# Sample key pages released by the count of projection chunks, six memory samples in two buffers, and two square roots moved on ScalarE

## The chip, the cores and the metric

The kernel runs on one core of a Trainium2 chip. Its time is the time on the device in microseconds (us), and the time of a version is the median of several runs.

## The reference

The kernel computes one layer of a decoder for a prompt of 256 tokens and for 8 samples of one token each. Both share the weights. Cut to what matters here:

```
h = rms_norm(x, norm1_w)
z = h @ w_in                                    # 2048 x 13312
zb, zc, zx, zq, zk, zv, zmq, zg = split(z)
y_conv = (zb * short_conv(zc * zx)) @ w_conv_out
q, k   = rope(rms_norm(zq)), rope(rms_norm(zk))
# prompt: attention over itself; sample: over 2048 cached positions (16 pages of 128) and itself
y_diff = subln(diff_attn(q, k_all, v_all)) @ w_diff_out
mk, mv = memory_kv(mem)                         # prompt: (rms_norm(mem) @ w_mem_kv), 256 memory rows
y_mem  = mem_attn(rms_norm(zmq), mk, mv) @ w_cross_out   # sample: its own cached 256 memory rows
x = x + (sigmoid(zg) * [y_conv, y_diff, y_mem]).sum() @ w_o
x = x + peer_ffn(rms_norm(x))                   # top 16 of 16384 experts for each of 8 heads, rows gathered
```

## The kernel before

All is fp32. The program is written engine by engine with semaphores; nothing is scheduled by a planner, so each engine and each DMA queue runs its list in the order in which it is written.

**Projections on TensorE.** `linear` computes z transposed in chunks of 128 columns for all 264 tokens. Four chunks make a cycle: `half_chunk(0, ...)` runs the first 8 of 16 contraction steps for the four chunks, and `half_chunk(1, ...)` the last 8. Each half reads one 2048 KB piece of weights in `wring`. SyncE fetches these pieces (`stream_halves`, `fetch_half`): the first half's buffer is refilled as soon as the four first halves are done, so its fetch runs during the second half of the cycle; the second half's buffer is refilled at the end of the cycle. `chunk_full` counts finished chunks, and it only moves in the second half of a cycle, once for each chunk. Chunks 1 to 8 are the queries, 9 to 16 the keys, 17 to 32 values and memory queries, 33 to 56 the three parts of the short convolution (`C_CONV` = 32). Then come 8 chunks of the prompt's memory (`C_MEM` = 56, 512 columns wide, L789), then the gates (L802, L814).

**Sample keys.** GpSimd's queue loads the 128 cached key pages, 512 KB each, in 32 groups of four (`load_pages`), into eight buffers: `kpages` 0 to 3 lie in `ring4`, 4 to 7 in `mkv`. A page is loaded when `kpage_used` says that the page eight before it was read. The index of the page is read from the table with `value_load`. VectorE multiplies a page by the broadcast query (L1510) and sums by head (L1515). Before each fourth group the query row of the next sample is loaded too.

**Memory scan.** After the pages, the 8 samples are scored against their cached memory in the same way (`score_memory`, L1540, L1543), two pages for a sample. `MEM_PAIR` says which pair of `kpages` a sample's two pages use. Each scored sample, of pages and of memory, moves `token_done`, which begins at 2; so 2+TS is the end of the page scan and 2+2*TS that of the memory scan (TS = 8).

**What waits for these.** The prompt's memory chunks are copied from PSUM into `mkv` by ScalarE (`memory_chunk`, L1190), and so can't be before the scan has left the pages in `mkv`. TensorE has four banks for the eight memory chunks, and chunk 5 needs chunk 1 taken. After chunk 8 TensorE runs `conv_state`, which needs VectorE's `conv_ready`, and `own_scores`, which needs all memory chunks taken.

**Roots.** VectorE's normalisations ask ScalarE for a square root: VectorE signals `sqrt_in` and waits for `sqrt_out` (L1473 is the instruction behind that wait); `root(n, ...)` on ScalarE is the other side. Root 3 belongs to the queries, root 4 to the keys and memory queries, root 5 to the prompt's memory keys.

The lines of the changed place:

```
for n in range(8):
    act.wait_ge(s["chunk_full"], C_QKV + 8 + n + 1)
    ...
    if n == 0:
        root(3, small[:, 3, 0:48])
...
conv_chunks(0, 5)
root(4, small[:, 3, 0:60])
conv_chunks(5, 1)
act.wait_ge(s["token_done"], 2 + 2 * TS)
```

Of the kernel before, what the change touches and what calls it, by code (L numbers as in the profile page):

```python
# [24 lines left out]
TP, TS = 256, 8  # L25
# [50 lines left out]
def build(nc, A, O):  # L76
# [17 lines left out]
    with ctx:  # L94
        def sb(name, shape, dt=F32):
            return ctx.enter_context(nc.sbuf_tensor("sb_" + name, shape, dt))

        def sem(name):
            return ctx.enter_context(nc.semaphore(name))
# [29 lines left out]

        kpages = [ring4[:, n, :] for n in range(4)] + [sq_mkv[:, n * DC:(n + 1) * DC] for n in range(4)]  # L130
        ring_flat = ring4[:, :, :].rearrange("p a b -> p (a b)")
        MEM_PAIR = [2, 3, 0, 1] * 2

        scores = cflat[:, 0:3 * 2 * PH * NKEY].rearrange("p (t n) -> p t n", t=3)
        work = S[:, :, :, :].rearrange("p a b c -> p (a b c)")
# [65 lines left out]
        small = sb("small", [P, 5, P])  # L201
# [18 lines left out]
        s = {n: sem(n) for n in names}  # L220
# [11 lines left out]
        C_QKV, C_CONV, C_MEM, C_O, C_PQ = 0, 32, 56, 64, 80  # L232
# [26 lines left out]
        def u_slot(g, j):  # L259
            return g * TOPK + j + dots_after(g, j - 1)  # L260
# [137 lines left out]
        def _(pool):  # L398
# [35 lines left out]
            pool.wait_ge(s["small_in"], 80)  # L434
            pool.wait_ge(s["xT_kept"], 16)

            def load_pages(i, g):

                par, half = g // 4 % 2, g % 2
                if g % 4 == 0:  # L440

                    b = i * 2 + g // 4
                    pool.wait_ge(s["token_done"], i * 2 + (g // 4 + 1))
                    pool.dma_start(qb[:, par, :], q_dram[ds(b, 1), :].to_broadcast([P, DC])).then_inc(qb_landed[par], 16)
                for r in range(4):
                    n = i * 32 + (g * 4 + r)
                    pool.wait_ge(s["kpage_used"], n + 1)
                    page = pool.value_load(pt[0:1, ds(n, 1)], min_val=0, max_val=POOL_PAGES - 1)
                    pool.dma_start(kpages[4 * half + r], cache_k[ds(page * PAGE, PAGE), :]).then_inc(k_landed[4 * half + r], 16)
# [5 lines left out]
            def load_query(b):  # L455
                pool.dma_start(qb[:, b % 2, :], mq_dram[b:b + 1, :].to_broadcast([P, DC])).then_inc(qb_landed[b % 2], 16)

            def load_memory(b):
                for t in range(2):
                    n = 2 * MEM_PAIR[b] + t  # L460
                    pool.dma_start(kpages[n], cmem_k[b * NM + t * P:b * NM + (t + 1) * P, :]).then_inc(k_landed[n], 16)
# [18 lines left out]
            for b in range(2, TS):  # L480
                pool.wait_ge(s["token_done"], 2 + TS + (b - 2) + 1)
                load_query(b)
                if b + 2 < TS:
                    load_memory(b + 2)

            def load_page(p):

# [100 lines left out]
            for g in range(2 * PH):  # L588
                pool.wait_ge(s["idx_ready"], g + 1)
                st(nc.gpsimd.tensor_copy(uidx[:, g % 4, :], idx_flat[:, g * TOPK:(g + 1) * TOPK]))  # L590
                for j in range(TOPK):
                    n = u_slot(g, j)
# [3 lines left out]
                    if dots_after(g, j) > dots_after(g, j - 1):  # L596
                        b = dots_after(g, j - 1)
# [498 lines left out]
        def _(act):  # L1096
# [10 lines left out]
            def root(n, ap):  # L1107
                act.wait_ge(s["sqrt_in"], n)
                st(A_(ap, ap, ACT.Sqrt))
                act.sem_inc(s["sqrt_out"], 1)  # L1110
# [44 lines left out]

            to_stage(8, C_QKV, R_QKV)
            act.wait_ge(s["rows_taken"], R_QKV + 8 + 2)
            for n in range(8):
                act.wait_ge(s["chunk_full"], C_QKV + 8 + n + 1)
                st(A_(zst[:, n % 2, :], ps[:, n % 4, 0:NT], ACT.Copy))  # L1160
                act.sem_inc(s["chunk_taken"], 1)
                if n == 0:
                    root(3, small[:, 3, 0:48])
                for k in (2 * n, 2 * n + 1):
                    act.wait_ge(s["xT_full"], KC + k + 1)
                    st(A_(memT[:, k, :], ps[:, 6 + k % 2, 0:NM], ACT.Copy, scale=cols[:, KC + k:KC + k + 1]))
                    act.sem_inc(s["xT_taken"], 1)
                act.wait_ge(s["tr_full"], R_QKV + 8 + n + 1)
                at = slice(DC + n * P, DC + (n + 1) * P)
                st.run(A_(rows[:, 0:2, at], ps[:, 4 + n % 2, 0:2 * P].rearrange("p (t n) -> p t n", t=2), ACT.Copy))  # L1170
                st(A_(rows[0:TS, 2, at], ps[0:TS, 4 + n % 2, 2 * P:3 * P], ACT.Copy))
                act.sem_inc(s["rows_taken"], 1)
            to_rows(16, C_QKV + 16, R_QKV + 16, rows, 2 * DC)

            def conv_chunks(i0, n):
                with st.loop(n, 4) as i:
                    for q in range(4):
                        act.wait_ge(s["chunk_full"], i * 4 + (C_CONV + 4 * i0 + q + 1))
                        st(A_(cflat[:, ds(i * (4 * NT) + (4 * i0 + q) * NT, NT)], ps[:, q, 0:NT], ACT.Copy))
                        act.sem_inc(s["chunk_taken"], 1)  # L1180

            conv_chunks(0, 5)
            root(4, small[:, 3, 0:60])
            conv_chunks(5, 1)

            act.wait_ge(s["token_done"], 2 + 2 * TS)
            def memory_chunk(n):
                g, t = n // 2, n % 2
                act.wait_ge(s["chunk_full"], C_MEM + n + 1)
# [191 lines left out]
        def _(dve):  # L1381
# [151 lines left out]
            def score_memory(b):  # L1533
# [3 lines left out]
                for t in range(2):  # L1537
                    n = 2 * MEM_PAIR[b] + t
                    dve.wait_ge(k_landed[n], 256 + 16 * (MEM_PAIR[:b].count(MEM_PAIR[b]) + 1))
                    st.run(TT(prods[t], kpages[n], qb[:, par, :], ALU.mult))  # L1540
# [556 lines left out]
```

## Time and profile before

| | before |
|---|---|
| median of 3 runs | 2750.24 us (2749.55 to 2758.01) |
| the profiled execution, its own time | 2760.93 us |
| its span | 2759.3 us |
| TensorE busy | 2447.8 us (89%) |
| VectorE busy | 1493.1 us (54%) |
| GpSimd busy | 907.5 us (33%) |
| ScalarE busy | 351.2 us (13%) |
| DMA | 919.23 MB, mean 333 GB/s |

The shares are averages over stages that differ much: until some 1400 us TensorE is busy nearly all the time, and after that the gathers of the experts fill the DMA engines. The time of a stage is read from that stage's own stretches and waits.

### The profile page before, as it was taken

Reading aid. Unit: us, or ns where it says so; the run is one execution under the profiler, and the core shown is the slowest. Engines: PE = TensorE matmul, PEld = TensorE weight load, DVE = VectorE, ACT = ScalarE, POOL = GpSimd, SP = SyncE. Lnnn points to the kernel's source line nnn. Section 1 sums busy time; section 2 is a strip of 40 time slices with the busy share of each in tenths; the row PEclk is TensorE's granted clock in tenths of the full one; section 3 lists DMA queues with packets and bytes.
Section 4 is the critical chain, followed back from the end, with each engine's and each line's share of the span. In section 5 each row is a group of like instructions: output and inputs, shape, how many; then the busy total and the mean of one; then the engine's idle time right before and its main releaser. Section 6 shows DMA issues by size and latency. Waiting matters only on the chain.

```text
span 2759.3 us, 27121 instructions
## 1 busy us (share of the span) xinstructions
PE 2447.8 (89%) x8853; PEld 1522.5 (55%) x8853; DVE 1493.1 (54%) x2370; ACT 351.2 (13%) x773; POOL 907.5 (33%) x889
## 2 busy tenths in 40 slices
PE   9999989999999999999997778776999597777777
PEld 7877778358766678888885233332434143323333
DVE  3499997713322223012377877884554665555543
ACT  2111000012222210001112101111011011111110
POOL 1122221100122210000056565655544564455542
PEclk9999999999999999999998999998989899999999
DMA  6599995754799975447398999999999999999998
GB/s 224 192 385 375 364 357 211 299 198 156 246 355 346 349 251 186 137 140 257 122 362 339 422 416 417 419 412 421 421 408 422 414 414 414 418 417 421 421 422 372
DMA packets 269027, 919.23 MB, mean 333 GB/s; under 512 B 15738, under 2 KB 122322, under 8 KB 199892
## 3 DMA queue, kind: packets, MB, share of 16 engines
q0 software_dynamic: 122448, 725.64, 65.5%
q1 hardware_dynamic: 146468, 192.20, 20.5%
q8 instruction: 59, 0.97, 0.1%
q14 instruction: 52, 0.43, 0.0%
HBM read 909.08 MB, written 8.72 MB: 333 GB/s over the span
## 4 chain that ended last, share of the span: by engine, by line
PE 47%; DMA 28%; DVE 12%; POOL 7%; issue 5%; ACT 0%; SPq 0%; DVEq 0%; POOLq 0%; ACTq 0%
DMA sb_bregion<-in_peer_u_dram,sb_ring 13%; PE ps L802 13%; PE ps L695 11%; PE ps L814 6%; DMA sb_wring<-in_w_in_dram 6%; PE ps L687 4%; PE ps L789 4%; DMA sb_mkv<-in_peer_u_dram,sb_ring 3%; DMA sb_S<-in_peer_u_dram,sb_ring 3%; DVE sb_bregion L1995 3%; PE ps L1051 3%; PE ps L902 2%; DVE sb_mkv L1995 2%; DMA sb_bregion<-in_peer_v_dram,sb_ring 1%; POOL sb_bregion L556 1%
## 5 line engine op out<-in xcount | busy, mean ns | idle before, releaser
L1051 PE MATMUL ps<-sb_wring,sb_ring 128*128 128x512 f32 x992 | 454.3, 607 | 85.3 <-DMA sb_wring<-in_peer_v_dram,sb_ring 84.7
L695 PE MATMUL ps<-sb_hT,sb_wring 128*128 128x264 f32 x1792 | 420.0, 395 | 24.7 <-DMA sb_wring<-in_w_in_dram 24.7
L1995 DVE CUSTOM_DVE_ANT_0 sb_bregion<-sb_bregion,sb_rows 128x2048 f32<-128x2048 f32 x128 | 293.5, 2293 | 214.8 <-DMA sb_bregion<-in_peer_u_dram,sb_ring 207.6
L695 PEld LDWEIGHTS ps<-sb_hT,sb_wring 128*128 128x128 f32 x1792 | 346.0, 195 | 88.7 <-issue 18.1
L1051 PEld LDWEIGHTS ps<-sb_wring,sb_ring 128*128 128x128 f32 x992 | 185.2, 193 | 352.3 <-issue 255.1
L802 PE MATMUL ps<-sb_hT,sb_wring 128*128 128x264 f32 x1536 | 365.5, 389 | 1.6 <-DVEq L1387 1.6
L802 PEld LDWEIGHTS ps<-sb_hT,sb_wring 128*128 128x128 f32 x1536 | 287.1, 190 | 64.9 <-issue 16.4
L1051 PE MATMUL ps<-sb_oreg,sb_ring 128*128 128x512 f32 x496 | 237.7, 630 | 75.3 <-DMA sb_oreg<-in_peer_v_dram,sb_ring 55.4
L1051 PE MATMUL ps<-sb_hT,sb_ring 128*128 128x512 f32 x496 | 231.7, 614 | 54.1 <-DMA sb_hT<-in_peer_v_dram,sb_ring 45.5
L556 POOL DMA_INDIRECT sb_bregion<-in_peer_u_dram,sb_ring x132 | 174.4, 1321 | 219.8 <-DVEq L1387 183.5
L1354 ACT ACTIVATE sb_ring<-sb_ident,sb_ring 128x128 f32<-128x128 f32 x248 | 99.6, 402 | 915.0 <-PE ps L1051 781.0
L1051 PEld LDWEIGHTS ps<-sb_oreg,sb_ring 128*128 128x128 f32 x496 | 97.1, 202 | 215.0 <-issue 154.9
L1995 DVE CUSTOM_DVE_ANT_0 sb_S<-sb_S,sb_rows 128x2048 f32<-128x2048 f32 x64 | 146.7, 2293 | 111.0 <-DMA sb_S<-in_peer_u_dram,sb_ring 107.9
L1995 DVE CUSTOM_DVE_ANT_0 sb_mkv<-sb_mkv,sb_rows 128x2048 f32<-128x2048 f32 x64 | 147.1, 2298 | 104.3 <-DMA sb_mkv<-in_peer_u_dram,sb_ring 99.6
L1051 PEld LDWEIGHTS ps<-sb_hT,sb_ring 128*128 128x128 f32 x496 | 93.2, 195 | 191.3 <-issue 150.1
L556 POOL DMA_INDIRECT sb_wring<-in_peer_v_dram,sb_ring x128 | 165.1, 1290 | 50.9 <-issue 40.4
L556 POOL DMA_INDIRECT sb_mkv<-in_peer_u_dram,sb_ring x66 | 101.0, 1530 | 190.5 <-DVEq L1387 176.7
L1515 DVE TENSOR_REDUCE sb_S<-sb_oreg 128x1024 f32 x128 | 149.5, 1208 | 0.0
L556 POOL DMA_INDIRECT sb_S<-in_peer_u_dram,sb_ring x66 | 94.8, 1436 | 86.0 <-DVEq L1387 59.0
L814 PE MATMUL ps<-sb_oreg,sb_bregion 128*128 128x264 f32 x512 | 122.1, 388 | 0.0
L590 POOL COPY sb_ring<-sb_ring 128x16 int32<-128x16 int32 x16 | 16.7, 1047 | 309.4 <-DVEq L1387 309.3
L789 PE MATMUL ps<-sb_wring,sb_bregion 128*128 128x512 f32 x256 | 111.8, 599 | 6.5 <-DMA sb_wring<-in_w_mem_kv_dram 6.5
(367 smaller groups left out, 2595.6 us busy)
## 6 DMA issues: line engine op xcount, KB each, us to landing
sb_wring<-in_w_in_dram SPq DMA_DIRECT2D x52, 2048.0 KB, 13.6
sb_ring<-in_cache_k_dram POOLq DMA_DIRECT2D x64, 512.0 KB, 7.6
sb_mkv<-in_cache_k_dram POOLq DMA_DIRECT2D x64, 512.0 KB, 7.2
sb_mkv<-in_cache_v_dram POOLq DMA_DIRECT2D x48, 512.0 KB, 7.1
sb_rows<-in_cache_v_dram POOLq DMA_DIRECT2D x47, 512.0 KB, 7.7
sb_wring<-in_w_mem_kv_dram SPq DMA_DIRECT2D x8, 2048.0 KB, 8.4
sb_wring<-in_w_o_dram SPq DMA_DIRECT2D x8, 2048.0 KB, 8.2
sb_S<-in_cache_v_dram POOLq DMA_DIRECT2D x22, 512.0 KB, 7.2
```

The costliest lines, as they stand in the source:

```text
L556: nc.gpsimd.indirect_dma_start(dst, None, table, bass.IndirectOffsetOnAxis(ap=idx, axis=0)).then_inc(landed, 16)
L590: st(nc.gpsimd.tensor_copy(uidx[:, g % 4, :], idx_flat[:, g * TOPK:(g + 1) * TOPK]))
L687: last = mm(ps[:, (2 * r + c) % 4, 0:NT], wring[:, r, k, c * P:(c + 1) * P], rhs[:, k, :], start=(k == 0), stop=(k == KC - 1))
L695: last = mm(ps[:, c, 0:NT], whalf[:, h, k % BC, c * P:(c + 1) * P], rhs[:, k, :], start=(k == 0), stop=(k == KC - 1))
L789: last = mm(ps[:, 2 * g + t, :], memT[:, k, t * P:(t + 1) * P], whalf[:, h, k % BC, :], start=(k == 0), stop=(k == KC - 1))
L802: last = mm(ps[:, c, 0:NT], wring[:, r, k, c * P:(c + 1) * P], hT[:, k, :], start=(k == 0), stop=(k == KC - 1))
L814: last = mm(ps[:, bank, 0:NT], bwring[:, r, k, c * P:(c + 1) * P], operand[:, k, :], start=(k == 0), stop=(k == BC - 1))
L902: last = mm(ps[g * QUAD:g * QUAD + w.shape[1], 6 + q, :], w, v_slots[page_slot(p)][:, q * 512:(q + 1) * 512], start=first, stop=final)
L1051: last = mm(ps[:, 4 * t + q, :], diag[:, k % 4, :], e_slots[v % ER][:, q * 512:(q + 1) * 512], start=False, stop=q_stop, skip_group_check= ...
L1354: st(A_(diag[:, k % 4, :], ident[:, :], ACT.Copy, scale=wexp[:, g % 4, j:j + 1]))
L1515: st.run(RED(out(p), by_head(prods[p % 2]), X, ALU.add))
L1995: st(V.tensor_tensor_reduce(out=u_slots[n % UR], in0=u_slots[n % UR], in1=h2, scale=1.0, scalar=0.0, op0=ALU.mult, op1=ALU.add, accum_out= ...
```

## The change

It has four parts.

1. **Pace.** Before each group g of `load_pages(i, g)`, GpSimd's queue also waits for `chunk_full` to reach i*11 + 11 + floor(11*(g-2)/8). In numbers, the 32 groups wait for chunks 8, 9, 11, 12, 13, 15, 16, 17, then the same plus 11 (19, 20, 22, 23, 24, 26, 27, 28), plus 22 (30 to 39) and plus 33 (41, 42, 44, 45, 46, 48, 49, 50).
2. **Pairs of the memory scan.** Samples 0 and 1 still use pairs 2 and 3 (in `mkv`); samples 2 to 7 take turns in pairs 0 and 1 (in `ring4`). The pages of samples 4 to 7 are therefore loaded when the sample two before them has been scored, where before they were loaded when the sample four before had been.
3. **Memory chunks.** ScalarE waits for `token_done` of 2+TS+2 (two memory samples scored) before it copies memory chunk 1, where it waited for 2+2*TS.
4. **Roots.** Root 3 stands ahead of key chunk 9 and no longer behind it. Root 4 stands behind all 24 convolution chunks and no longer ahead of the last four.

```diff
-        MEM_PAIR = [2, 3, 0, 1] * 2
+        MEM_PAIR = [2, 3] + [0, 1] * 3
...
+            PACE = 11
+
             def load_pages(i, g):
...
                     pool.dma_start(qb[:, par, :], q_dram[ds(b, 1), :].to_broadcast([P, DC])).then_inc(qb_landed[par], 16)
+                pool.wait_ge(s["chunk_full"], i * PACE + (C_QKV + 11 + PACE * (g - 2) // 8))
                 for r in range(4):
...
                 load_query(b)
-                if b + 2 < TS:
-                    load_memory(b + 2)
+                if b >= 4:
+                    load_memory(b)
...
             act.wait_ge(s["rows_taken"], R_QKV + 8 + 2)
+            root(3, small[:, 3, 0:48])
             for n in range(8):
                 act.wait_ge(s["chunk_full"], C_QKV + 8 + n + 1)
                 st(A_(zst[:, n % 2, :], ps[:, n % 4, 0:NT], ACT.Copy))
                 act.sem_inc(s["chunk_taken"], 1)
-                if n == 0:
-                    root(3, small[:, 3, 0:48])
...
-            conv_chunks(0, 5)
+            conv_chunks(0, 6)
             root(4, small[:, 3, 0:60])
-            conv_chunks(5, 1)
-
-            act.wait_ge(s["token_done"], 2 + 2 * TS)
+
+            act.wait_ge(s["token_done"], 2 + TS + 2)
```

ScalarE, between the last query chunk and the first key chunks; L1160 (L1164 in the changed kernel) copies a key chunk out of PSUM, L1109 (L1112) is the root. Before:

```order
L69 COMPARE_AND_BRANCH
L1160 ACTIVATE sb_zst<-ps 128x264 [waits chunk_full,rows_taken]
L1109 ACT_TABLE_LOAD [waits act_done]
L1109 ACTIVATE sb_small<-sb_small 128x48 [waits sqrt_in]
L1166 ACTIVATE sb_bregion<-ps,sb_cols 128x256 [waits act_done,xT_full] x2
L1170 ACTIVATE sb_rows<-ps 128x2x128 [waits act_done,tr_full]
```

And now:

```order
L69 COMPARE_AND_BRANCH
L1112 ACT_TABLE_LOAD [waits sqrt_in]
L1112 ACTIVATE sb_small<-sb_small 128x48 [waits rows_taken]
L1164 ACTIVATE sb_zst<-ps 128x264 [waits act_done,chunk_full]
L1168 ACTIVATE sb_bregion<-ps,sb_cols 128x256 [waits act_done,xT_full] x2
L1172 ACTIVATE sb_rows<-ps 128x2x128 [waits act_done,tr_full]
```

The root and its table load moved ahead of the first key chunk; nothing else moved here.

GpSimd's queue, the memory scan's loads behind the stores of the prompt's keys and values; `mq_rows_scratch` is the memory query row of one sample, `in_cache_mem_k_dram` two pages of its memory. Before:

```order
L475 DMA out_v_prompt_dram<-sb_rows 128x2x1024
L477 DMA out_v_sample_dram<-sb_rows 8x1024
L456 DMA sb_oreg<-mq_rows_scratch 128x1024 [waits token_done]
L461 DMA sb_mkv<-in_cache_mem_k_dram 128x1024 x2
L456 DMA sb_oreg<-mq_rows_scratch 128x1024 [waits token_done]
L461 DMA sb_mkv<-in_cache_mem_k_dram 128x1024 x2
L456 DMA sb_oreg<-mq_rows_scratch 128x1024 [waits token_done]
L461 DMA sb_ring<-in_cache_mem_k_dram 128x1024 x2
L456 DMA sb_oreg<-mq_rows_scratch 128x1024 [waits token_done]
L461 DMA sb_ring<-in_cache_mem_k_dram 128x1024 x2
L456 DMA sb_oreg<-mq_rows_scratch 128x1024 [waits token_done] x2
```

And now:

```order
L478 DMA out_v_prompt_dram<-sb_rows 128x2x1024
L480 DMA out_v_sample_dram<-sb_rows 8x1024
L459 DMA sb_oreg<-mq_rows_scratch 128x1024 [waits token_done] x3
L464 DMA sb_ring<-in_cache_mem_k_dram 128x1024 x2
L459 DMA sb_oreg<-mq_rows_scratch 128x1024 [waits token_done]
L464 DMA sb_ring<-in_cache_mem_k_dram 128x1024 x2
L459 DMA sb_oreg<-mq_rows_scratch 128x1024 [waits token_done]
L464 DMA sb_ring<-in_cache_mem_k_dram 128x1024 x2
L459 DMA sb_oreg<-mq_rows_scratch 128x1024 [waits token_done]
L464 DMA sb_ring<-in_cache_mem_k_dram 128x1024 x2
```

The four pairs of pages moved two samples later in the queue, and all go to `ring4`.

## Rows read from the trace of the kernel before

**Rows 1.** Stretch of the gates to the scores: length, busy of each engine, PEclk, DMA, GB/s

```profile
595.00:1400.00 805.00, 801.77 (x4046) 629.81 (x4047) 211.52 (x468) 123.31 (x250) 94.76 (x163) 1.00 0.68 237
```

**Rows 2.** Stretches by cycle of four chunks; last columns PEclk, DMA share, GB/s

```profile
147.40:184.70 37.30, 33.48 (x146) 27.71 (x144) 36.88 (x33) 4.64 (x14) 9.07 (x18) 0.91 1.02 396
...
219.60:250.80 31.20, 29.99 (x142) 25.20 (x141) 30.78 (x28) 3.69 (x12) 7.51 (x15) 1.00 1.01 379
250.80:283.00 32.20, 29.93 (x141) 25.16 (x140) 31.26 (x29) 3.69 (x12) 7.96 (x15) 1.00 0.98 372
283.00:312.80 29.80, 29.42 (x135) 24.46 (x132) 29.80 (x27) 2.63 (x8) 7.78 (x15) 1.00 1.00 373
312.80:348.70 35.90, 30.57 (x128) 25.50 (x128) 35.48 (x33) 1.62 (x5) 8.69 (x17) 0.90 0.97 357
...
447.60:476.00 28.40, 28.40 (x129) 24.27 (x128) 18.63 (x17) 1.82 (x5) 6.17 (x11) 1.00 0.59 202
```

**Rows 3.** TensorE's waits, 120 to 480 us, and two of them in the timeline

```profile
PE ps L695 <- DMA sb_wring<-in_w_in_dram: 24.3, 9, 5.3
```

```profile
267.84 7.39 PE L695 MATMUL ps<-sb_hT,sb_wring 128*128 128x264 f32 x32 [2.27 <-DMA sb_wring<-in_w_in_dram]
...
317.95 30.57 PE L695 MATMUL ps<-sb_hT,sb_wring 128*128 128x264 f32 x128 [5.27 <-DMA sb_wring<-in_w_in_dram]
```

**Rows 4.** DMA issues of weights, median us to landing, 53 to 116 us

```profile
sb_wring<-in_w_in_dram SPq DMA_DIRECT2D x5, 2048.0 KB, 7.9
```

**Rows 5.** The same, weights and pages, 131 to 419 us

```profile
sb_wring<-in_w_in_dram SPq DMA_DIRECT2D x17, 2048.0 KB, 17.1
...
sb_ring<-in_cache_k_dram POOLq DMA_DIRECT2D x60, 512.0 KB, 7.8
```

**Rows 6.** Timeline of VectorE around root 3 and the first page

```profile
105.25 0.45 DVE L1473 RECIPROCAL sb_small<-sb_small 128x48 f32<-128x48 f32 x1 [11.72 <-ACTq L1110]
...
128.09 1.23 DVE L1510 TENSOR_TENSOR sb_oreg<-sb_ring,sb_oreg 128x1024 f32<-128x1024 f32 x1 [12.40 <-DMA sb_ring<-in_cache_k_dram]
```

**Rows 7.** VectorE's page multiplies from `ring4`: ns min/median/max, first and last start

```profile
L1510 DVE TENSOR_TENSOR sb_oreg<-sb_ring,sb_oreg x64: 1210/1216/1226, 128.1 to 411.3; 128x1024 f32<-128x1024 f32 x64
```

**Rows 8.** Timeline of GpSimd: first page of groups 10 and 24

```profile
205.59 0.53 POOL L449 DMA_DIRECT2D sb_ring<-in_cache_k_dram  x1 [4.02 <-DVEq L1387]
...
334.28 0.53 POOL L449 DMA_DIRECT2D sb_ring<-in_cache_k_dram  x1 [1.36 <-DVEq L1387]
```

**Rows 9.** Timeline of ScalarE: copies of chunks 22 and 41

```profile
212.80 0.39 ACT L1148 ACTIVATE sb_zst<-ps 128x264 f32<-128x264 f32 x1 [0.18 <-ACT sb_rows L1153]
...
372.48 0.39 ACT L1179 ACTIVATE sb_conv<-ps 128x264 f32 x1 [23.44 <-PE ps L695]
```

**Rows 10.** Timelines of ScalarE and VectorE around root 4

```profile
448.29 0.25 ACT L1109 ACTIVATE sb_small<-sb_small 128x60 f32<-128x60 f32 x1 [0.25 <-ACT sb_conv L1179]
```

```profile
448.62 0.53 DVE L1473 RECIPROCAL sb_small<-sb_small 128x60 f32<-128x60 f32 x1 [10.47 <-ACTq L1110]
```

**Rows 11.** VectorE's memory scan: first multiplies of sample 4; last sums

```profile
505.07 2.36 DVE L1540 TENSOR_TENSOR sb_oreg<-sb_mkv,sb_oreg 128x1024 f32<-128x1024 f32 x2 [1.51 <-DMA sb_oreg<-mq_rows_scratch]
...
524.61 2.34 DVE L1543 TENSOR_REDUCE sb_Sm<-sb_oreg 128x4 f32<-128x1024 f32 x2
```

**Rows 12.** ScalarE: first copy of memory chunks, root 5, first copy behind it

```profile
527.04 1.49 ACT L1190 ACTIVATE sb_mkv<-ps,sb_stat 128x512 f32<-128x512 f32 x2 [50.61 <-DVEq L1387]
...
554.74 0.21 ACT L1109 ACTIVATE sb_small<-sb_small 128x8 f32<-128x8 f32 x1 [14.89 <-DVEq L1387]
```

**Rows 13.** The page's DMA issues: memory pages, median us to landing

```profile
sb_mkv<-in_cache_mem_k_dram POOLq DMA_DIRECT2D x8, 512.0 KB, 11.7
```

**Rows 14.** TensorE in the memory chunks and at the first gate chunk

```profile
475.84 13.90 PE L789 MATMUL ps<-sb_wring,sb_bregion 128*128 128x512 f32 x32
496.20 97.86 PE L789 MATMUL ps<-sb_wring,sb_bregion 128*128 128x512 f32 x224 [6.46 <-DMA sb_wring<-in_w_mem_kv_dram]
...
595.29 7.39 PE L802 MATMUL ps<-sb_hT,sb_wring 128*128 128x264 f32 x32
```

## The prediction, on record before the changed kernel ran

> **What bounds the kernel now.** I read the stretches by engine first, then TensorE's waits, then the landings of the DMAs that end them. From the gates to the scores TensorE is busy 801.77 of 805.00 us at a granted clock of 1.00 [rows 1]. What shortens the time up to the first gate chunk at 595.29 us [rows 14] is therefore worth its full size there, and the gathers behind it start by so much earlier, unless some later transfer needed the time. So the question is when the first gate chunk starts.
>
> Up to there TensorE loses time while key pages are loaded. The stretches by cycle show it: a cycle of four chunks takes 28.40 us at the end, when no page is in flight, and 37.30, 31.20, 32.20, 29.80, 35.90 us in the scan [rows 2]. A clean cycle of the first 32 chunks is 31.20 less its one wait of 1.2, or 29.9; 32.20 less 2.27 says the same [rows 2, 3]. The first convolution cycle is 29.5. The ten cycles from 147.40 to 476.00 would take 4 x 29.9 + 29.5 + 5 x 28.4 = 291.1 us clean and take 328.6. **The loss is 37.5 us**, of which 24.3 us are nine waits for weights [rows 3], and the rest is slow running behind the long ones: the stretch with the wait of 5.27 has a granted clock of 0.90, the one with 2.27 has 1.00 [rows 2, 3]. A wait of 2 us costs itself, one of 5 us about 7.
>
> Why the weights are late: a piece of 2048 KB lands 7.9 us after its issue when nothing else moves [rows 4] and 17.1 us in the scan [rows 5], and its due time is half a cycle, 14.2 to 15 us. Pages are read by VectorE at (411.3 - 128.1) / 123 = 2.30 us each [rows 7], 9.2 us a group, so 3.1 groups in a clean cycle.
>
> **Root 3.** VectorE waits 11.72 us for root 3, from 93.53 to 105.25 [rows 6], because ScalarE first waits for key chunk 9. In the new order only the table load and the root lie between, about 1.8 us from the same row's neighbours, so the query rows, their way through DRAM and the first page come some 9.9 us earlier: first multiply at 118.2 in place of 128.09 [rows 6]. ScalarE was idle there; the cost is nothing. But it isn't a gain by itself: VectorE is not what TensorE waits for. It brings the first collision one cycle forward, into the piece fetched at some 116 us. I charge the 7.4 us that the first cycle with pages loses now (37.30 - 29.9) [rows 2] to the new first one, and 2 us (bounds 0 and 5) to the next, since the pace doesn't hold in either.
>
> **Pace.** Groups ask for 11 chunks in 8 groups, 1.375 chunks of 7.1 us or 9.8 us a group in a clean run, against 9.2 by VectorE. It doesn't hold for the first ten groups. Group 10 was issued at 205.59 and would now wait for chunk 22, copied at 212.80; group 24 was issued at 334.28 and would wait for chunk 41, copied at 372.48 [rows 8, 9]. So the pages fall back behind the chunks, to three groups in a cycle and two in the cycles of chunks 29 to 32 and 49 to 52. All are released in the second half of a cycle, at chunk 1 of it at the earliest. The piece fetched at the start of that half has 3.6 us and the page's own latency to itself, half of its 7.9 us [rows 4]; the rest shared as now at half speed gives some 12 us of the 14.2. The piece fetched at the end of the cycle meets what is left of the second group and the whole third. In bytes a conv cycle now wants 4.2 MB of weights, 6.3 of pages and 0.4 of query rows, 10.9 MB in 28.4 us or 384 GB/s, against 372 to 396 GB/s moved in the busiest cycles [rows 2]. That is tight. Bounds: no wait at all, or two in three of the later cycles with 2.3 us each and a slow one (15 us in all). I take 6 us, nearest to the row with 2.27, since a wait that short left the clock alone.
>
> Sum for the end of the convolution chunks: 37.5 - 7.4 - 2 - 6 = **22.1 us earlier**, at 453.9.
>
> **Root 4.** It now stands behind chunk 56: 453.9 + 1.0 (as 448.62 stands to the end of chunk 52 at 447.60 [rows 2, 10]). VectorE asks for it 26.9 us after the last multiply from `ring4` (438.15, from 448.62 - 10.47, less 411.3) [rows 7, 10]. Group 30 is released by chunk 49 at 414.8, its page lands by 7.8 us [rows 5], four pages take 6.9: VectorE asks at about 456. Root and request meet; the reciprocal comes at 456, 7.4 us later than now.
>
> **Memory scan.** Samples 2 to 7 live on two pairs. Now four samples take 526.95 - 505.07 = 21.9 us, 5.5 each [rows 11]. With the load issued when the sample two before is done, a sample takes half of landing plus scoring: (7.8 + 4.7) / 2 = 6.25 [rows 5, 11]; over four samples +3. The memory pages' median is 11.7 [rows 13]; that is the upper end, 8.2 each and +16 over six samples; the lower end is 0. The scan ends at 526.95 + 7.4 + 3 = 537.4. Two samples are done by some 491, and TensorE's chunk 5 of the memory begins at 453.9 + 55.9 = 509.8, so the new `token_done` wait holds nobody. With the old one ScalarE would free a bank only at about 537 and TensorE would wait 27 us: the gain of the pace hangs on this edit. Root 5 follows the scan's end by 27.8 us [rows 11, 12]: 565.2, and three copies of 0.75 stand behind it, 567.7.
>
> **TensorE's own end.** 453.9 + 13.90 + 97.86 + its weight wait. That wait of 6.46 us [rows 14] falls into the burst of stores and memory pages; four pages fewer lie in it, the fetch comes at the same place in the burst. Bounds 0 and 6.5; I take 3.2. Memory chunks end at 568.9, the first gate chunk starts 1.2 us later as now, at 570.1. VectorE and ScalarE are ready at 567.7, so TensorE decides, by little. **595.3 - 570.1 = 25 us gained.** The profiled execution's 2760.9 becomes 2736; the shown runs have their median 10.7 us lower, and the same 25 us off 2750.24 gives 2725.
>
> **Rivals.** A difference under 0.3% (8 us) is no change to a measurement of this kernel.
> B, late pieces stay in part. Three of the later cycles keep a collision like the conv cycles' (35.90 less 28.4 or 29.5, about 6.7 each, 20 us in place of 6) [rows 2]. For it: 384 GB/s against what was moved. Against: two cycles have only two groups and a head start is real. Gain 11, **2739**. The Trainium skill has a rule on its side (DMA: Bandwidth & Descriptors, "Queues, rings and completion order"): an engine takes turns between its queues packet by packet, so a piece fetched into waiting pages gets its fixed share however the pages were paced. By that rule the pace helps only as far as pages are not in flight.
> C, nothing is won. Pages and weights are the same bytes, the DMA engines are full (share 0.97 to 1.02 in the scan [rows 2]), and TensorE still ends its chunks at 476; the other edits then have nothing to free. Against: from 447.60 on the share is 0.59 [rows 2], room that the later pages can use. **2750**.
> D, slower: VectorE's chain becomes the bound. With C's 476, the root comes at 477, 28.4 later, and the scan at 16 us over: 526.95 + 28.4 + 16 = 571.3. It decides from a scan's end of 595.3 - 31.9 = 563.4 on; `own_scores` then waits 8 to 11 us. **2760**. It needs both C and the slow landings.
>
> **Chances.** Forecast 0.70 (own range 2714 to 2733), B 0.16, C 0.10, D 0.04. Faster: the forecast and three quarters of B, 0.82; within 0.3%: 0.14; slower 0.04. The range 2713 to 2741 holds the forecast and most of B. Its low end is every bound at its good side: 37.5 - 7.4 and no other loss, 6.5 of the memory wait, 36.6 less; the VectorE chain then stops it near 35.
>
> **What would show it.** First multiply of a page at about 118. A new wait of some 4 us near 131, and none above 3 us after 230. Page issues waiting for TensorE from about 207 on. Last convolution chunk at 454 (450 to 462). Reciprocal behind root 4 at 456 with a short wait. Memory samples 2 to 7 at some 6.3 us. First gate chunk at 570, busy shares from there to the gathers as now. I am wrong if waits of 4 to 5 us go on between 280 and 420, if TensorE waits at `own_scores`, or if the gather stage gives back what was won.

## The result: slower by 0.9%, and the profile after

The changed kernel takes 2774.80 us (median of 5 runs, 2771.33 to 2777.57) against 2750.24 us (5 runs, 2749.12 to 2758.01). The ratio is 1.0088, with a 95% interval of 1.0067 to 1.0108. I had forecast 2725 us, with a range of 2713 to 2741.

| | before | after |
|---|---|---|
| span of the profiled execution | 2759.3 us | 2773.2 us |
| last of the 56 chunks ends | 476.0 us | 487.3 us |
| waits for weights in the scan, 120 to 480 us | 24.3 us | 32.3 us |
| first gate chunk starts | 595.3 us | 609.2 us |

The spans differ by 13.9 us, and so do the starts of the first gate chunk. From there on nothing is given back or lost. The stretch of the gates, 805 us long and 14 us later, has the busy times of [rows 1]:

```profile
609.00:1414.00 805.00, 801.77 (x4047) 630.06 (x4047) 211.49 (x469) 123.12 (x250) 92.32 (x163) 1.00 0.68 237
```

So that step of the prediction holds, and the question is what happened before 609 us. TensorE's waits from 120 to 480 us, as the first row of [rows 3], and then stretches of the changed kernel by cycle of four chunks, as [rows 2] (columns: length, busy of TensorE, weight loads, VectorE, ScalarE, GpSimd, then PEclk, DMA share, GB/s):

```profile
PE ps L698 <- DMA sb_wring<-in_w_in_dram: 32.3, 9, 4.6
```

```profile
115.10:153.90 38.80, 34.60 (x158) 28.93 (x157) 36.21 (x32) 7.47 (x20) 10.93 (x21) 0.91 1.00 384
...
222.10:258.50 36.40, 32.64 (x142) 27.05 (x141) 27.46 (x25) 3.68 (x12) 6.87 (x13) 0.91 0.83 306
...
293.90:323.00 29.10, 29.10 (x135) 24.86 (x134) 20.79 (x19) 2.62 (x8) 5.33 (x11) 1.00 0.88 320
323.00:357.90 34.90, 30.34 (x130) 25.35 (x129) 27.88 (x25) 1.56 (x4) 6.90 (x14) 0.95 0.85 319
...
422.90:458.80 35.90, 31.82 (x130) 26.39 (x129) 26.94 (x25) 1.56 (x4) 6.41 (x13) 0.90 0.83 308
458.80:487.30 28.50, 28.50 (x130) 24.35 (x129) 27.95 (x18) 1.56 (x4) 2.54 (x5) 1.00 0.76 281
```

In the middle four of these rows the DMA share is 0.83 to 0.88 and 306 to 320 GB/s, where it was 0.97 to 1.02, yet three of the cycles take 34.9 to 36.4 us, as long as the worst of [rows 2]. So over a cycle the DMA engines are no longer full, and the weights still come late. The chain of the work that ended last shows which piece is late (start, us, what): it is each time the one fetched at the end of a cycle.

```profile
222.25 18.45 DMA sb_wring<-in_w_in_dram
258.71 18.49 DMA sb_wring<-in_w_in_dram
323.18 18.59 DMA sb_wring<-in_w_in_dram
358.09 17.50 DMA sb_wring<-in_w_in_dram
392.01 16.39 DMA sb_wring<-in_w_in_dram
423.12 18.10 DMA sb_wring<-in_w_in_dram
```

GpSimd's timeline shows where the pages went. These are the first and the last page of the three groups of one cycle, and the first page of the next cycle:

```profile
252.13 0.53 POOL L452 DMA_DIRECT2D sb_mkv<-in_cache_k_dram  x1 [20.63 <-issue]
...
257.42 0.53 POOL L452 DMA_DIRECT2D sb_ring<-in_cache_k_dram  x1 [0.86 <-issue]
...
262.71 0.53 POOL L452 DMA_DIRECT2D sb_mkv<-in_cache_k_dram  x1 [0.86 <-issue]
...
266.63 0.53 POOL L452 DMA_DIRECT2D sb_mkv<-in_cache_k_dram  x1 [0.77 <-issue]
...
287.47 0.53 POOL L452 DMA_DIRECT2D sb_ring<-in_cache_k_dram  x1 [19.32 <-issue]
```

All twelve pages are issued from 252.13 to 266.63, about the piece of weights that is fetched at 258.71. Then no page is issued for 21 us. The profile names no releaser for these gaps; that the count makes them is shown by e2 below, where it is gone and no two pages lie over 5.2 us apart. The DMA share in the stretches around it says the same: idle for a third of the time ahead of that fetch, full while it is under way.

```profile
240.70:250.80 10.10, 10.06 (x34) 8.16 (x35) 7.85 (x7) 0.39 (x1) 0.00 (x0) 0.73 0.61 227
250.80:258.70 7.90, 7.90 (x41) 6.70 (x39) 1.63 (x2) 1.84 (x6) 2.64 (x5) 1.00 0.68 202
258.70:277.20 18.50, 14.74 (x69) 12.25 (x67) 18.50 (x17) 1.45 (x5) 4.23 (x8) 0.99 0.99 383
```

The other steps that the change touches, in VectorE's and TensorE's timelines: root 3 comes early, root 4 hardly makes VectorE wait, samples 4 and later wait for their pages, and TensorE waits twice for memory weights.

```profile
94.65 0.45 DVE L1474 RECIPROCAL sb_small<-sb_small 128x48 f32<-128x48 f32 x1 [1.75 <-ACTq L1113]
...
115.23 1.22 DVE L1511 TENSOR_TENSOR sb_oreg<-sb_ring,sb_oreg 128x1024 f32<-128x1024 f32 x1 [10.13 <-DMA sb_ring<-in_cache_k_dram]
...
488.41 0.53 DVE L1474 RECIPROCAL sb_small<-sb_small 128x60 f32<-128x60 f32 x1 [0.77 <-ACTq L1113]
...
544.84 2.36 DVE L1541 TENSOR_TENSOR sb_oreg<-sb_ring,sb_oreg 128x1024 f32<-128x1024 f32 x2 [2.22 <-DMA sb_ring<-in_cache_mem_k_dram]
```

```profile
487.15 41.36 PE L792 MATMUL ps<-sb_wring,sb_bregion 128*128 128x512 f32 x96
534.45 30.30 PE L792 MATMUL ps<-sb_wring,sb_bregion 128*128 128x512 f32 x64 [5.94 <-DMA sb_wring<-in_w_mem_kv_dram]
566.52 41.47 PE L792 MATMUL ps<-sb_wring,sb_bregion 128*128 128x512 f32 x96 [1.77 <-DMA sb_wring<-in_w_mem_kv_dram]
```

The 13.9 us of the spans are 11.3 us at the end of the chunks, 1.3 us of waits for memory weights (5.94 + 1.77 less 6.46) and 1.3 us of slow running behind them (the last by difference). The medians differ by 24.6 us, not by 13.9. The profiled execution of before (2760.9) lies 10.7 us over its median, that of the changed kernel (2774.8) on it; the experiments come back to that.

### The profile page after: what moved, and what is told of

Same layout as the page of the kernel before. It is cut to its first block, busy times and chain, and to the rows that moved or that the text cites. A ratio compares the mean times of both kernels' runs of the same rounds, so it can differ in the third digit from the quotient of the medians.

```text
span 2773.2 us, 27164 instructions
## 1 busy us (share of the span) xinstructions
PE 2447.4 (88%) x8853; PEld 1523.5 (55%) x8853; DVE 1494.5 (54%) x2370; ACT 350.8 (13%) x773; POOL 900.1 (32%) x889
## 4 chain that ended last, share of the span: by engine, by line
PE 46%; DMA 30%; DVE 12%; POOL 6%; issue 5%; ACT 0%; DVEq 0%; POOLq 0%; SPq 0%; ACTq 0%
DMA sb_bregion<-in_peer_u_dram,sb_ring 13%; PE ps L805 13%; PE ps L698 10%; PE ps L817 6%; DMA sb_wring<-in_w_in_dram 6%; DMA sb_mkv<-in_peer_u_dram,sb_ring 4%; PE ps L690 4%; PE ps L1054 3%; PE ps L792 3%; DMA sb_S<-in_peer_u_dram,sb_ring 3%; DVE sb_bregion L1996 3%; PE ps L905 2%; DVE sb_mkv L1996 2%; DMA sb_bregion<-in_peer_v_dram,sb_ring 1%; POOL sb_wring L559 1%
## 5 line engine op out<-in xcount | busy, mean ns | idle before, releaser
L698 PE MATMUL ps<-sb_hT,sb_wring 128*128 128x264 f32 x1792 | 424.2, 398 | 32.3 <-DMA sb_wring<-in_w_in_dram 32.3
L805 PEld LDWEIGHTS ps<-sb_hT,sb_wring 128*128 128x128 f32 x1536 | 287.2, 190 | 64.8 <-issue 16.4
L559 POOL DMA_INDIRECT sb_mkv<-in_peer_u_dram,sb_ring x66 | 94.7, 1435 | 193.2 <-DVEq L1388 169.0
L690 PE MATMUL ps<-sb_conv,sb_wring 128*128 128x264 f32 x512 | 116.4, 386 | 0.0
## 6 DMA issues: line engine op xcount, KB each, us to landing
sb_wring<-in_w_in_dram SPq DMA_DIRECT2D x52, 2048.0 KB, 10.7
```

Of the source, the lines that this page charges most:

```text
L559: nc.gpsimd.indirect_dma_start(dst, None, table, bass.IndirectOffsetOnAxis(ap=idx, axis=0)).then_inc(landed, 16)
L690: last = mm(ps[:, (2 * r + c) % 4, 0:NT], wring[:, r, k, c * P:(c + 1) * P], rhs[:, k, :], start=(k == 0), stop=(k == KC - 1))
L698: last = mm(ps[:, c, 0:NT], whalf[:, h, k % BC, c * P:(c + 1) * P], rhs[:, k, :], start=(k == 0), stop=(k == KC - 1))
L805: last = mm(ps[:, c, 0:NT], wring[:, r, k, c * P:(c + 1) * P], hT[:, k, :], start=(k == 0), stop=(k == KC - 1))
```

## The experiments

The theory, P: the count of chunks moves only in the second half of a cycle, so the pace lets all pages of a cycle go within some 15 us, around the fetch of the second half's weights, and that fetch is late in nearly each cycle. Its rivals: R, the early root 3 adds a collision; T, the bytes need their time however they are spread; L, the late root 4 puts the memory scan onto the memory weights. All ratios are against runs of the kernel before on the same chip. They are estimated from all runs of both kernels, so they are not quite the quotient of two medians. The kernel before has a median of 2748.46 to 2752.78 us by chip, so that medians from different chips are comparable to some 4 us; e1 to e4 share a chip, e5 to e8, e9 to e12, and e13 and e14.

| run | median us | ratio (95% interval) | end of chunks | waits in scan | first gate |
|---|---|---|---|---|---|
| e1 before again (one run) | 2758.25 | | 473.5 | 23.4 | 592.5 |
| e2 no pace | 2756.15 | 1.0023 (0.9996 to 1.0049) | 466.9 | 17.9 | 591.8 |
| e3 pace only | 2788.52 | 1.0130 (1.0071 to 1.0190) | 482.9 | 28.5 | 623.5 |
| e4 even count, 22 | 2754.18 | 1.0015 (0.9991 to 1.0038) | 459.6 | 14.0 | 582.2 |
| e5 root 3 only | 2754.19 | 1.0004 (0.9985 to 1.0023) | 474.0 | 22.6 | 594.6 |
| e6 pairs and wait only | 2749.60 | 1.0010 (0.9986 to 1.0033) | 463.8 | 19.1 | 585.0 |
| e7 no pace, root 4 old | 2751.88 | 1.0007 (0.9990 to 1.0024) | 462.4 | 17.0 | 583.6 |
| e8 even count, 22, root 4 old | 2753.81 | 1.0011 (0.9993 to 1.0030) | 465.3 | 17.6 | 589.9 |
| e9 count in first halves | 2753.63 | 1.0019 (1.0000 to 1.0037) | 461.0 | 16.9 | 585.0 |
| e10 quarter pages (one run) | 2744.22 | | 437.2 | 0.0 | 575.6 |
| e11 even count, 22, roots old | 2758.16 | 1.0025 (1.0012 to 1.0038) | 473.1 | 22.4 | 599.5 |
| e12 even count, 20, roots old | 2744.85 | 0.9979 (0.9957 to 1.0001) | 456.5 | 12.3 | 579.5 |
| e13 chunk count, 10, roots old | 2772.10 | 1.0063 (1.0039 to 1.0087) | 483.6 | 29.2 | 608.9 |
| e14 even count, 20, root 3 early | 2744.03 | 0.9961 (0.9936 to 0.9986) | 457.2 | 12.2 | 579.4 |

**e1, the kernel before once more.**

> The kernel before, unchanged, for a second profile. Its five shown times stand in two groups (2749 to 2750 and 2757 to 2758 us) and its profiled execution took 2760.9 us. If the groups differ in the scan of the key pages, this profile has other waits for weights than the 24.3 us of the first one; if they differ in the gathers at the end, the first gate chunk starts at 595 us again and the rest moves.

Its span is 2756.5 us, its gate chunk starts at 592.5. The stretch behind that is 2164.0 us long in both profiles of before and in the changed kernel's. Nine waits for weights stand at nearly the same places, but their lengths differ: 2.9 us at 235.2 in place of 1.2, 3.9 at 315.4 in place of 5.3. So the scan is where these executions differ.

**e2, without the pace.**

```diff
-                pool.wait_ge(s["chunk_full"], i * PACE + (C_QKV + 11 + PACE * (g - 2) // 8))
```

> The changed kernel without the new wait on the chunk count; the pairs, the memory chunks' wait and both roots stay changed. Theory P (the pace puts the pages of a cycle onto the fetch of the second half's weights): waits for weights fall back to 24 us or so, the first gate chunk starts at 590 to 597 us and the time is 2745 to 2755. Rival R (root 3 early starts the pages a cycle earlier and so adds a collision): the waits stay near 30 us, the gate chunk at 603 or later, time 2765 or more.

The gate chunk comes at 591.8, as P has it, and the median is 18.6 us under the changed kernel's. The time is 1 us over P's range, and the waits fall further than P said, to 17.9 us. R's numbers didn't come; the early root costs no such sum. VectorE, done with the pages at 411.6, then stood 39.74 us before the late root 4, as its timeline shows:

```profile
467.96 0.53 DVE L1473 RECIPROCAL sb_small<-sb_small 128x60 f32<-128x60 f32 x1 [39.74 <-ACTq L1112]
```

**e3, the pace alone.**

```diff
+                pool.wait_ge(s["chunk_full"], i * 11 + (C_QKV + 11 + 11 * (g - 2) // 8))
                 for r in range(4):
```

> The kernel before with the new wait on the chunk count alone. Theory P: in each cycle from chunk 21 on, the second half's weights land 16 us or more after their issue and TensorE waits 2.5 to 4.5 us there, last convolution chunk at 480 to 490; the scan ends late, and with the old wait for the whole memory scan TensorE waits for a bank at memory chunk 5: 2780 to 2795. Rival R: nothing but the late scan, last convolution chunk at 470 to 477.

As P has it, and it is some 12 to 14 us slower than the whole change. TensorE's timeline shows what the edit of the memory chunks' wait is for: with the old wait TensorE stands 16.83 us before memory chunk 5 until ScalarE may copy.

```profile
531.95 16.90 PE L790 MATMUL ps<-sb_wring,sb_bregion 128*128 128x512 f32 x32 [6.38 <-DMA sb_wring<-in_w_mem_kv_dram]
565.68 56.60 PE L790 MATMUL ps<-sb_wring,sb_bregion 128*128 128x512 f32 x128 [16.83 <-ACTq L1192]
```

**e4, the same pace by half chunks.** A new count moves at the last matmul but one of each half chunk, eight times in a cycle.

```diff
                     last = mm(ps[:, c, 0:NT], whalf[:, h, k % BC, ...], rhs[:, k, :], ...)
+                    if k == (h + 1) * BC - 2:
+                        last.then_inc(s["half_chunks"], 1)
...
-                pool.wait_ge(s["chunk_full"], i * PACE + (C_QKV + 11 + PACE * (g - 2) // 8))
+                pool.wait_ge(s["half_chunks"], i * 22 + (22 + 22 * (g - 2) // 8))
```

> The changed kernel, but the pages wait for a count that moves at each half chunk, so eight times in a cycle and evenly, in place of four times in its second half; the mean rate is the same (22 half chunks for 8 groups). Theory P: what matters is when in the cycle the pages are released; no piece meets three groups, waits for weights fall under 15 us, last convolution chunk before 468, first gate chunk before 588, time 2725 to 2745. Rival T (the same bytes need the time however they are spread; the DMA engines are full): waits stay at 25 to 32 us, time within 5 us of the changed kernel.

Rate and all other parts are those of the change; only the evenness differs. Waits fall from 32.3 to 14.0 us, the gate chunk comes 27 us earlier, the median is 20.6 us lower. T falls. The time itself is over the 2725 to 2745 that I gave: it isn't faster than before, and only 2 us under e2, which has no pace at all. So evenness takes away the loss that the change made; that a pace at this rate gains anything isn't shown.

**e5 and e6, the other parts alone.**

```diff
+            root(3, small[:, 3, 0:48])
             for n in range(8):
...
-                if n == 0:
-                    root(3, small[:, 3, 0:48])
```

> The kernel before with root 3 ahead of the first key chunk, nothing else. If the early root is harmless (theory P), the first page is multiplied near 117 us, the scan ends some 10 us earlier, waits for weights stay at 23 to 25 us, only one cycle earlier, and the time is that of before within 5 us. Rival R: the added cycle of collision is a loss of its own, waits of 28 us or more, first gate chunk 4 us or more later.

The pages start 12 us earlier and nothing is won or lost that can be measured.

```diff
-        MEM_PAIR = [2, 3, 0, 1] * 2
+        MEM_PAIR = [2, 3] + [0, 1] * 3
...
-                if b + 2 < TS:
-                    load_memory(b + 2)
+                if b >= 4:
+                    load_memory(b)
...
-            act.wait_ge(s["token_done"], 2 + 2 * TS)
+            act.wait_ge(s["token_done"], 2 + TS + 2)
```

> The kernel before with the pairs of the memory scan and the memory chunks' wait changed, both roots and the pages as before. Samples 4 to 7 wait for their pages: their multiplies at 6.3 to 7 us from one another in place of 5.8; TensorE isn't held either way, since it reaches memory chunk 5 late enough. Time within 5 us of before. If these parts cost by themselves, the wait for memory weights or a wait at the last memory chunk is over 5 us longer than the 6 us of before.

No difference in time either; samples 4 to 7 take 25.4 us, 6.4 each, as expected. But this profile is of use beside those of before: up to the end of the chunks the program is the same, and the chunks end at 463.8 here, at 476.0 and 473.5 in the two profiles of before.

**e7 and e8, root 4 back in its old place**, without the pace and with the even one.

```diff
-            conv_chunks(0, 6)
+            conv_chunks(0, 5)
             root(4, small[:, 3, 0:60])
+            conv_chunks(5, 1)
```

> As the run without the pace, and root 4 back ahead of the last four convolution chunks. Theory L (late root 4 is what took the rest: VectorE waited 39.7 us for it, and the burst of the memory scan fell on TensorE's memory weights): the wait becomes 8 us or less at about 440, the memory scan starts some 25 us earlier, TensorE's memory stage has under 8 us of waits and the first gate chunk starts before 588. Rival M: the memory scan is hidden anyway; gate chunk within 2 us of 591.8.

> As the run with the even count of half chunks, and root 4 back ahead of the last four convolution chunks. VectorE asks for it at about 446 while ScalarE is free until chunk 53, so the wait of 12.4 us goes and the scan of the memory starts 13 us earlier. Theory L: first gate chunk at 576 to 580, time 2 to 6 us under the run with the even count. Rival M: gate chunk at 582 again.

Without the pace, root 4 is waited for 8.4 us in place of 39.7, and the gate chunk comes 8.2 us earlier. But 4.5 of these lie ahead of the chunks' end, where root 4 has no part: from there to the gate chunk it is 121.2 us in place of 124.9, so at most 3.7 us are root 4's. The median is 4.3 us lower, which is inside the spread of the runs. With the even pace it went the other way: the chunks end 5.7 us later in e8, the stretch behind them is 124.6 us in place of 122.6, and the medians are 0.4 us apart. What root 4 costs when the scan ends early stays unsettled within some 5 us. In the changed kernel VectorE waited 0.77 us for it.

**e9, a count that moves in the first half.**

```diff
-                pool.wait_ge(s["chunk_full"], i * PACE + (C_QKV + 11 + PACE * (g - 2) // 8))
+                pool.wait_ge(s["half_chunks"], i * PACE + (C_QKV + 11 + PACE * (g - 2) // 8))
...
+                    if k == BC - 2:
+                        last.then_inc(s["half_chunks"], 1)
```

> The changed kernel, but the pages wait for a count that moves at the end of each first half chunk, so in the first half of a cycle only; thresholds are the same numbers. Theory P says that the pages fall on whatever piece is fetched at the end of the half in which they are released: now the pieces issued in the middle of a cycle should land after 16 us or more, those issued at its end after 8 to 12, the waits of 2.5 to 4.5 us move from the middle to the start of cycles, and the time stays 10 us or more above before (2762 to 2780). Rival T (full DMA engines): both pieces at 13 to 17 us as before.

The late piece changed places: from 290 us on the chain of the work that ended last holds the pieces fetched in the middle of a cycle.

```profile
291.37 16.58 DMA sb_wring<-in_w_in_dram
322.76 17.11 DMA sb_wring<-in_w_in_dram
356.37 15.52 DMA sb_wring<-in_w_in_dram
386.70 16.92 DMA sb_wring<-in_w_in_dram
```

The piece issued between 305 and 306.5 us, at a cycle's end, landed in 9.2 us, by the DMA issues of that stretch:

```profile
sb_wring<-in_w_in_dram SPq DMA_DIRECT2D x1, 2048.0 KB, 9.2
```

In the changed kernel it is the reverse: 18.5 us for the piece issued at 258.7, and for the one issued in the middle of the next cycle, between 273 and 275 us:

```profile
sb_wring<-in_w_in_dram SPq DMA_DIRECT2D x1, 2048.0 KB, 10.9
```

So when in the cycle the pages go decides which piece is late. But the time is 8 us under what I expected, level with the even e4, though this count is as uneven as that of the change. The marks come half a cycle earlier here, so the first gap of over 15 us between pages ends at 281 us; from 200 to 276 us the pieces took 9 to 14 us and nothing waited. Of the 15.4 us of waits that e9 has less than the changed kernel, 11.3 lie ahead of 281 us. In the four cycles with bunches behind that, the waits are 10.4 us, against 14.5. So bunched pages make a piece late in either half, and an uneven count costs by the number of cycles in which it really holds pages back.

**e10, a quarter of the page traffic.** It loads 256 of the 1024 columns of each key page; the lines that first fill five of the buffers once are left out here.

```diff
-                    pool.dma_start(kpages[4 * half + r], cache_k[ds(page * PAGE, PAGE), :]).then_inc(...)
+                    pool.dma_start(kpages[4 * half + r][:, 0:DC // 4], cache_k[ds(page * PAGE, PAGE), 0:DC // 4]).then_inc(...)
```

> The kernel before, but of each key page only the first 256 of 1024 columns are loaded (so the sample scores are of other keys), after one full load of the five buffers that nothing else has filled; page traffic is a quarter and VectorE's work is the same. It measures what all page traffic costs TensorE. By the sum of the prediction a clean run ends its convolution chunks at 438 to 440 us; every piece lands in 8 to 11 us, no wait. If waits stay, the loss isn't of the pages.

The ten cycles in one stretch (columns as above): 291.10 us, a granted clock of 1.00, the very sum that the prediction has for a clean run. VectorE's work is there in full (285.29 us busy), so the pages' traffic is all of the loss.

```profile
146.10:437.20 291.10, 291.10 (x1339) 248.36 (x1338) 285.29 (x247) 26.34 (x79) 65.49 (x122) 1.00 0.62 214
```

TensorE then waits 16.53 us for ScalarE at memory chunk 5, since the old wait stands here:

```profile
516.48 57.86 PE L793 MATMUL ps<-sb_wring,sb_bregion 128*128 128x512 f32 x128 [16.53 <-ACTq L1195]
```

**e11 and e12, the even pace with both roots old, at two rates.** The first is e8 with root 3 back behind key chunk 9. The second also has

```diff
-                pool.wait_ge(s["half_chunks"], i * 22 + (22 + 22 * (g - 2) // 8))
+                pool.wait_ge(s["half_chunks"], i * 20 + (30 + 20 * (g - 2) // 8))
```

> The even count of half chunks with the pairs and the memory chunks' wait of the change, and both roots where they were. Theory P: last convolution chunk at 455 to 462, first gate chunk at 577 to 584, time 2738 to 2748, the first version under before; rival V (the loss that a profile of before shows is larger than in its other runs, so there is little to win): 2746 to 2754, no difference.

> As the one before it, with 20 half chunks for 8 groups in place of 22 (and a later start of the count, 26 half chunks before the second group's), 9.0 us a group in a clean run, under VectorE's 9.2: the pages are held only where TensorE has been late. Theory P: like the kernel before in its landings, 13 to 17 us, and within 5 us of it; if the mean rate matters more than the evenness, it lies between before and the run with 22.

e11 is slower than before, and V and P were both too low for it. e12 is 13.3 us better and the first at or under before; its interval still holds 1. Single pieces still take up to 18.4 us here, but TensorE waits only five times. Of its rate and its later start, which does it isn't told apart.

**e13, e12 with the count of chunks.**

```diff
-                pool.wait_ge(s["half_chunks"], i * 20 + (30 + 20 * (g - 2) // 8))
+                pool.wait_ge(s["chunk_full"], i * 10 + (C_QKV + 14 + 10 * (g - 2) // 8))
```

> The run with 20 half chunks for 8 groups, but counted in chunks (10 for 8 groups, each group released within three half chunks of the other run's mark), so in the second half of a cycle alone; pairs, memory wait and both roots are the same as there. If the evenness is what matters (theory P), the pieces issued at a cycle's end land after 16 us or more and those issued in its middle after 8 to 11, waits are 22 us or more, last convolution chunk after 465, time 2753 to 2768. If the mean rate and the late start of the count made that run good (rival Q), the waits stay at 10 to 16 us and the time at 2742 to 2750.

Its median is 27.3 us over e12's, by the ratios some 23 us, and 4 us over P's range. Waits rise from 12.3 to 29.2 us, and these four rows of the chain are again of the piece at a cycle's end (those of the middle took 7.7 to 13.0 us):

```profile
283.52 19.84 DMA sb_wring<-in_w_in_dram
320.81 18.86 DMA sb_wring<-in_w_in_dram
356.05 18.31 DMA sb_wring<-in_w_in_dram
390.46 16.23 DMA sb_wring<-in_w_in_dram
```

```profile
PE ps L698 <- DMA sb_wring<-in_w_in_dram: 29.2, 10, 5.0
```

With the rate and the roots alike, and each mark within three half chunks of e12's (one half chunk earlier on average), release in the second half of the cycle costs over 20 us. Q falls.

**e14, e12 with root 3 early.**

> The run with 20 half chunks for 8 groups, with root 3 early as in the change. The first groups come 10 us earlier and are held by the count from the second on. If the early root costs only by the collision at the start of the scan, and the count now prevents that, this is no slower than 2744.9 (2738 to 2748); if the early start costs anyway, a wait of 3 us or more stands near 133 and the time is 2747 to 2755.

2744.03 us, ratio 0.9961 (0.9936 to 0.9986): the first version whose interval lies under 1, by 0.4%, and 31 us under the changed kernel. It is the best of thirteen versions, the kernel before has its highest median on this chip, and e12 differs from it by 0.8 us, so I take the 0.4% as likely and not as shown. TensorE waits four times in the scan:

```profile
PE ps L698 <- DMA sb_wring<-in_w_in_dram: 12.2, 4, 3.9
```

A stretch of it, for comparison with the cycles of the changed kernel; the DMA engines are full and TensorE loses nothing:

```profile
199.00:230.00 31.00, 31.00 (x147) 26.40 (x146) 26.81 (x24) 3.87 (x13) 7.64 (x15) 1.00 0.98 365
```

## Why the prediction was wrong, point by point

**The clean run and the loss: right for that execution.** 291.1 us clean is what e10 takes. But I took 37.5 us as the loss to be won back, from one execution that lies 10.7 us over the median. In e6 the same instructions lose 25 us up to the same point (463.8 in place of 476.0). A base from the slow end made the loss look larger by about 10 us. I had the two numbers side by side and only subtracted.

**Root 3: right.** First multiply at 115.2, where I had 118. The first collision came one cycle forward and cost 38.8 - 31.6 = 7.2 us, with e10's cycle as the clean one (I charged 7.4), the next cycle 33.1 - 29.9 = 3.2 (I charged 2).

**The step that failed: the 6 us for the piece that is fetched at the end of a cycle.** The prediction gave the piece of the middle a head start, and let the other meet "what is left of the second group and the whole third", for 6 us in all. From 115.1 to 487.3 the changed kernel takes 372.2 us, against 322.7 in e10 (114.5 to 437.2). The loss is 49.5 us, of which 10.4 are the first two cycles: **39 us in place of 6**. The head start was there (the middle pieces landed in 7.9 to 10.9 us). What the late piece meets was right too: behind the fetch at 258.71 come three pages of the second group and the four of the third. Its price was wrong. Most cycles have three groups whose marks are three of the four chunks of its second half (22 to 24, 26 to 28, 33 to 35, 37 to 39), GpSimd needs 1.3 us to issue a page and 5.3 a group, and so the twelve pages go within 14.5 to 17.4 us around the cycle's end. The fetch then took 16.4 to 18.6 us, over the half cycle of 14.2 to 15 that it has, and TensorE waited 2.4 to 4.6 us in seven of the nine cycles behind the first two; in six of the seven the granted clock is 0.90 to 0.95. The only clean ones are those behind the two cycles with two groups (29.10 and 28.50 us). I had charged the average: bytes per cycle (384 GB/s wanted) against what the engines can carry, and one wait of 2.27 us as the model for the rest.

The sum for the gate chunk goes wrong by the same term: 609.2 in place of 570.1 is 33.4 us at the end of the chunks, 4.5 at the memory weights and 1.2 that I can't place. No version came near the 25 us: the best two, e12 and e14, lie 3.7 and 8.8 us under before in the median.

**The upper bound was too low.** I gave 15 us for "two in three of the later cycles with 2.3 us each and a slow one". The right bound was at hand in [rows 2]: every cycle as slow as 35.9. Rival B had the mechanism, a fetch among waiting pages takes its 17 us however the pages were paced: the late pieces shown took 16.4 to 18.6 us in the changed kernel at a DMA share of some 0.83 over the cycle, 15.5 to 17.1 in e9, 16.2 to 19.8 in e13. That fits the rule that it names of the Trainium skill (DMA: Bandwidth & Descriptors, "Queues, rings and completion order"), that a DMA engine takes turns between its queues packet by packet; the turns themselves no run here shows. I gave B 0.16 and priced it at three cycles; it was nearly all of them, and then it is slower than before. That case, B in every cycle, I had not made a rival; it is what the side "slower" should have been.

**Pace, root 4, memory scan, TensorE's end.** The pace held pages from the eighth group on (issued at 177.04 after a gap of 13.57 us), where I had said that the first ten go free: I had compared the marks with the page times of before, without the 9.9 us by which I let the early root move them (group 7 stood at 177.11 before). Root and request met, with 0.77 us of wait. Samples 4 to 7 took 24.2 us against 21.9, where I had 25 (upper end 33). The new wait for two samples held TensorE nowhere, and e3 and e10 show what the old one would have cost, 16.8 and 16.5 us, where I had 27. The memory weights' waits were 7.7 us, where I had 3.2, above my bound of 6.5. Small beside the 33 us of the pace.

**Rival D** named another chain; in the changed kernel VectorE's chain didn't decide. **C** fell with e4 and e12: the same bytes can pass with less loss (chunks' end at 459.6 and 456.5).

## What to carry to other kernels

When transfers are released by a count, write out at which moments the count moves and lay the critical fetches beside them; a mean rate says nothing about what each fetch meets. Release by a count that moves evenly: here that took some 20 us off the bunched one, twice (e4, and e12 against e13). It isn't a gain by itself, for the even pace at 22 half chunks is level with no pace at all (e4 and e2). And before a loss is read from one profile, see where that execution lies among the runs: here a third of the loss that was to be won wasn't there in a profile from near the median (e6).

## What the runs showed that I had not expected

The same instructions lose 25 to 38 us in the scan from one execution to the next (chunks' end at 463.8, 473.5, 476.0), and the runs of the kernel before reach from 2738 to 2776 us. The three profiles are from different chips, but the runs on one chip alone reach from 2741 to 2776 us. The five runs of the changed kernel lie within 6.2 us, the five of before beside them within 8.9; that the bunched pace makes executions more alike isn't shown. Why executions differ isn't settled; the profiles show only that the waits differ in length, and in e6 also in place. And the DMA share can fall from 1.0 to 0.83 over cycles while the fetch that counts is as late as ever.
